# Two expert chunks issued during the attention, a separate region for one of them, and two raw buffers for the last four weight halves

## The chip, the cores and the metric

The kernel runs on one core of one Trainium2 chip. The metric is the device time of one execution in microseconds (us); lower is better. The figures for the kernel before are three runs and one more execution that the hardware profiler recorded.

## The reference, cut to what matters

One transformer layer for 256 tokens of width 1024, all in float32: a gated linear attention and a gating unit side by side, then cross-attention to 256 memory rows, then a mixture of 32 experts.

```
x = x + (gate_a * y_a + gate_b * y_b) @ w_mix_out[l]
mem_n = _rmsnorm(mem, norm_mem_g[l])
x = x + _cross_attn(_rmsnorm(x, norm_x_g[l]), mem_n, w_xq[l], w_xk[l], w_xv[l], w_xo[l])
x = x + _moe(_rmsnorm(x, norm_ffn_g[l]), w_router[l], b_router[l], w_e1[l], b_e1[l], w_e2[l], b_e2[l])
```

`_cross_attn` computes, for four heads of width 256, `softmax(q k^T / 16) v` and multiplies the heads by `w_xo`. `_moe` takes the four best experts of each token; each expert is two matrices, `w_e1[e]` (1024 x 2048) and `w_e2[e]` (1024 x 1024), 12.6 MB together, with a clipped gate between them. All 32 experts are computed, so about 403 MB of expert weights are read in every execution.

## The kernel before, in words

The program has one hand-written instruction list per engine. Semaphores alone order the engines among each other; each engine, and the DMA queue that SP (SyncE) issues, goes through its own list in order.

**The dense part.** The weights of the dense matrices come in 21 pieces (`PIECES`), each of two halves of 1 MB, so 42 halves with numbers n from 0 to 41. Piece `xq1` is halves 36 and 37, `xo0` is 38 and 39, `xo1` is 40 and 41. SP loads half n into one of four raw buffers (`load_half`, profile line L352). ScalarE (ACT) copies it with rounding into a "high" part (`high_part`, L548), GpSimd (POOL) computes the "low" part as the difference (`low_part`, L466) and increments `low_made`, and TensorE (PE) multiplies with both parts (L1224 and L1268). A raw buffer is free again when the low part of the half in it is done, so with `N_RAW_SLOTS` = 4 half n is issued when `low_made` has reached n - 3. The pairs of high and low parts have three buffers of their own, so `high_part(n)` also waits until PE has used half n - 3.

**The attention.** PE computes the scores of heads 0 to 3 (L1413), VectorE (DVE) takes the row maximum (L1018) and scales it with a small operation on `stat` (L1021), ACT takes the exponentials (`soft`, L689), DVE multiplies the probabilities by the reciprocal sums (L1028), PE transposes them (L1202) and multiplies them with the values (`attend`, L1430). In ACT's list the order around the change is: high part 39, two copies, high part 40, `soft(2)`, `soft(3)`. Half 41 has its high part after the four heads. Then PE multiplies by `xo0` and `xo1` (L1224), normalises, computes the router and begins the experts.

**The experts.** An expert is six chunks of 2 MB: c = 0 to 3 of the first matrix (PE at L1551) and 4, 5 of the second (PE at L1584). Eight chunk slots are reused in turn: one is the memory rows' old buffer, one lies in `shared`, two are the four raw buffers taken in twos (`raw_slot(1)` is raw buffers 2 and 3, `raw_slot(0)` is 0 and 1), and four are the old pair buffers and hT. Two more places serve only once, for chunks 3 and 4 of expert 0 (`EXTRA_CHUNKS`). Chunk 3 goes to `from_glu`, the region of `shared` in which the experts' activations will lie. Before, that region overlaps the probabilities of the attention. Chunk 4 goes in two halves to `sgu_vectors` and `side`. SP issues a chunk into a reused slot when PE has used what was in it (`chunk_was_used`); all chunk issues show as L367, chunk 3 as L416.

SP's list before, from half 37 on: halves 38 to 41, each behind its `low_made`; chunk 0 once PE has filled group `vm11`; chunk 1 once `ao3`, the last head, is filled; chunk 3; chunk 2; chunk 5 when all 42 low parts are done; chunks 6 to 9 as the output projection ends; the two halves of chunk 4; then the slots in turn.

Of the kernel before, what the change touches and what calls it, by code (L numbers as in the profile page):

```python
# [44 lines left out]

PIECE_HALF = DC * HALF // 2
N_RAW_SLOTS = 4
N_PAIR_SLOTS = 3
HALF_CHUNK = 2 * D
CHUNK = 2 * HALF_CHUNK  # L50
# [7 lines left out]
EXTRA_CHUNKS = (W1_CHUNKS - 1, W1_CHUNKS)  # L58
# [3 lines left out]
PIECES = ["qk", "v", "r", "sv", "u", "ga0", "ga1", "gb0", "gb1", "pa", "pb", "xk0", "xk1",  # L62
          "mx0", "mx1", "xv0", "xv1", "xq0", "xq1", "xo0", "xo1"]
# [29 lines left out]
def bank_of(group):  # L93
    return INDEX[group] % N_BANKS
# [10 lines left out]
def use_of(group):  # L105

    return INDEX[group] // N_BANKS + 1


def layer_program(nc, a, out):  # L110
    with ExitStack() as ctx:
        def sb(name, shape, dt=F32):
            return ctx.enter_context(nc.sbuf_tensor(name, shape, dt))

        def sem(name):
            return ctx.enter_context(nc.semaphore(name))
# [3 lines left out]

        raw = sb("raw", [P, N_RAW_SLOTS * PIECE_HALF])
        with ExitStack() as early:
            def early_sb(name, shape):
                return early.enter_context(nc.sbuf_tensor(name, shape, F32R))


            pairs = early_sb("pairs", [P, N_PAIR_SLOTS, 2, DC // 2, HALF])
            hT = early_sb("hT", [P, 2, DC, T])
            memT = early_sb("memT", [P, 2, DC, T])

        late = sb("late", [P, 2 * N_PAIR_SLOTS * PIECE_HALF + 4 * DC * T])
        with ExitStack() as early:
# [38 lines left out]
        at = [0]  # L171

        def carve(cols, p=P):
            v = shared[0:p, at[0]:at[0] + cols]
            at[0] += cols
            assert at[0] <= 13 * 1024, at[0]
            return v

        def cut(v, *dims):
            if len(dims) == 2:  # L180
                return v.rearrange("p (a b) -> p a b", a=dims[0])
            return v.rearrange("p (a b c) -> p a b c", a=dims[0], b=dims[1])
# [48 lines left out]
        putT = cut(carve(TT * P), TT, P)  # L231
        gathered = carve(HALF)
        xeT = cut(carve(HALF), 4, P)
        glu_at = at[0]
        glu = carve(HALF)
        lin = carve(HALF)
# [3 lines left out]
        from_glu = shared[:, glu_at:glu_at + CHUNK]  # L240
# [8 lines left out]
        bank_emptied = [sem(f"bank_emptied{b}") for b in range(N_BANKS)]  # L249
        raw_full = [sem(f"raw_full{b}") for b in range(N_RAW_SLOTS)]  # L250
        extra_full = [sem(f"extra_full{b}") for b in range(len(EXTRA_CHUNKS))]
# [12 lines left out]
        s = {n: sem(n) for n in names}  # L264

        block = ctx.enter_context(nc.Block())


        def raw_half(n):
            k = n % N_RAW_SLOTS  # L270
            return raw[:, k * PIECE_HALF:(k + 1) * PIECE_HALF]

        def raw_arrived(eng, n):
            eng.wait_ge(raw_full[n % N_RAW_SLOTS], 16 * (n // N_RAW_SLOTS + 1))

        def pair(m):
            return pairs[:, m % N_PAIR_SLOTS]

        def split_used(eng, m):

            if m % 2 == 0:
                eng.wait_ge(s["first_half_used"], m // 2 + 1)
            else:
                filled(eng, LAST_USE[PIECES[m // 2]])
# [8 lines left out]
        HALVES = 2 * len(PIECES)  # L293
        pair_order = [m % N_PAIR_SLOTS for m in range(HALVES - N_PAIR_SLOTS, HALVES)]
        hT_slot, memT_slot = N_PAIR_SLOTS, N_PAIR_SLOTS + 1

        chunk_slots = ([late_slot(memT_slot), shared[:, 0:CHUNK], raw_slot(1), raw_slot(0)]
                       + [late_slot(q) for q in pair_order] + [late_slot(hT_slot)])
        assert len(chunk_slots) == N_CHUNK_SLOTS and 2 * PIECE_HALF == CHUNK == 2 * DC * T
        assert (HALVES - N_RAW_SLOTS) % N_RAW_SLOTS == 2  # L300

        def turn_of(c):

# [3 lines left out]
        def slot_of(c, step_is_first):  # L307
            return (turn_of(c) if step_is_first else c - len(EXTRA_CHUNKS)) % N_CHUNK_SLOTS
# [15 lines left out]
        def filled(eng, group):  # L324
            eng.wait_ge(bank_filled[bank_of(group)], use_of(group))
# [6 lines left out]
        def piece_source(name):  # L332
            def cols(w, lo):
                return w.rearrange("(c p) n -> p c n", p=P)[:, :, lo:lo + HALF]
            lows = {"qk": 0, "v": OFF_V, "r": OFF_R, "u": OFF_U, "sv": OFF_SV, "ga0": OFF_G,
                    "ga1": OFF_G + HALF, "gb0": OFF_G + D, "gb1": OFF_G + D + HALF}
            if name in lows:
                return cols(w_in[0], lows[name]), DC
            if name in ("pa", "pb"):
                return a["w_proj_a" if name == "pa" else "w_proj_b"][0].rearrange("(c p) n -> p c n", p=P), DC // 2  # L340
            w = {"xk": "w_xk", "xv": "w_xv", "mx": "w_mix_out", "xq": "w_xq", "xo": "w_xo"}[name[:2]]
            return cols(a[w][0], HALF * int(name[2])), DC

        @block.sync
        def _(sp):
            def load_half(n):
                if n >= N_RAW_SLOTS:

                    sp.wait_ge(s["low_made"], n - N_RAW_SLOTS + 1)
                src, c = piece_source(PIECES[n // 2])  # L350
                src = src[:, (n % 2) * (c // 2):(n % 2 + 1) * (c // 2), :]
                sp.dma_start(raw_half(n).rearrange("p (c n) -> p c n", c=c // 2), src).then_inc(  # L352
                    raw_full[n % N_RAW_SLOTS], 16)

            def chunk_source(c, e):

                k = c % CHUNKS
                if k < W1_CHUNKS:
                    rows_ = a["w_e1"][0, e, k * W1_SUB * P:(k + 1) * W1_SUB * P, :]
                    return rows_.rearrange("(p i) n -> p (i n)", i=W1_SUB)  # L360
                k -= W1_CHUNKS
                rows_ = a["w_e2"][0, e, k * W2_SUB * P:(k + 1) * W2_SUB * P, :]
                return rows_.rearrange("(p i) n -> p (i n)", i=W2_SUB)

            def load_chunk(c, e, step_is_first=False):
                slot = slot_of(c, step_is_first)
                sp.dma_start(chunk_slots[slot], chunk_source(c, e)).then_inc(chunk_full[slot], 16)  # L367
# [13 lines left out]
            sp.dma_start(wa2[:], a["gla_w_a2"][0]).then_inc(s["wa2_in"], 16)  # L381
            sp.dma_start(router_bias[:], a["b_router"][0:1, :].to_broadcast([P, N_EXP])).then_inc(s["wr_in"], 16)
            load_half(0)
            load_half(1)
            load_half(2)
# [7 lines left out]
            for n in range(N_RAW_SLOTS, HALVES):  # L393
                load_half(n)
                if n == 2 * PIECES.index("xk0"):

                    filled(sp, "o1")
                    for q in range(4):
                        cols = a["b_e1"][0].rearrange("e (h j n) -> e h j n", h=2, j=2)[:, :, q // 2, :]
                        sp.dma_start(b1_rows[N_EXP * q:N_EXP * (q + 1), :].rearrange("e (h n) -> e h n", h=2),  # L400
                                     cols).then_inc(s["b1_in"], 16)
                if n == 2 * PIECES.index("xv1"):

                    filled(sp, "kT0")
                    sp.wait_ge(s["sv_normed"], 2)
                    sp.dma_start(g_ffn, a["norm_ffn_g"][0:1, :].to_broadcast([P, D])).then_inc(s["gffn_in"], 16)
                    sp.dma_start(g_final, a["norm_final_g"].rearrange("(a d) -> a d", a=1).to_broadcast(
                        [P, D])).then_inc(s["gfin_in"], 16)
                    sp.dma_start(b2, a["b_e2"][0]).then_inc(s["b2_in"], 16)

            filled(sp, "vm11")
            load_chunk(0, 0, True)
            filled(sp, "ao3")
            load_chunk(1, 0, True)
            sp.wait_ge(s["b1_split"], 1)
            sp.dma_start(from_glu, chunk_source(EXTRA_CHUNKS[0], 0)).then_inc(extra_full[0], 16)  # L416
            sp.wait_ge(s["low_made"], HALVES - 2)
            load_chunk(2, 0, True)
            sp.wait_ge(s["low_made"], HALVES)
            load_chunk(5, 0, True)  # L420
            filled(sp, "x210")
# [16 lines left out]
            n = sp.value_load(trips[0:1, 0:1], min_val=GROUPS_OF_EXPERTS, max_val=ROUNDS * GROUPS_OF_EXPERTS)  # L438
# [15 lines left out]
        def _(pool):  # L454
# [7 lines left out]
            def low_part(m):  # L462

                pool.wait_ge(s["high_made"], m + 1)
                high, low = (pair(m)[:, i].rearrange("p c n -> p (c n)") for i in range(2))
                g.tensor_tensor(low, raw_half(m), high, ALU.subtract).then_inc(s["low_made"], 1)  # L466
# [35 lines left out]
        def _(sc):  # L502
# [41 lines left out]
            def high_part(m):  # L544
                if m >= N_PAIR_SLOTS:
                    split_used(sc, m - N_PAIR_SLOTS)
                raw_arrived(sc, m)
                A.activation(pair(m)[:, 0].rearrange("p c n -> p (c n)"), raw_half(m), ACT.Copy).then_inc(  # L548
                    s["high_made"], 1)
# [1065 lines left out]
```

## Time and profile before

| what | value |
|---|---|
| runs | 1243.12, 1241.75, 1241.39 us; median 1241.75 us |
| the profiled execution | 1242.61 us, its span 1240.9 us |
| TensorE busy | 1162.9 us, 94% of the span |
| VectorE, ScalarE, GpSimd busy | 347.0, 279.0, 205.1 us |
| HBM read | 451.79 MB, 365 GB/s over the span |

The span runs from the first to the last instruction of the program; the 1.7 us between it and the time lie around it. The page cuts the span into 40 slices of 31 us. In them the DMA rate is 136 to 313 GB/s up to slice 9, 430 in slice 10, 333, 377 and 413 in the next three, and 427 to 430 from there almost to the end:

```
GB/s 313 170 204 136 178 179 199 192 140 430 333 377 413 430 427 427 429 429 428 428 429 428 427 429 429 429 428 429 428 427 429 428 427 429 430 429 427 429 428 210
```

The dense part ends and the experts begin at about 315 us.

### The profile page before, as it was taken

The numbers are of one execution on the slowest core, as the hardware profiler recorded it, in microseconds if no ns is written. First come the engines' busy times: TensorE is split into PE (matmuls) and PEld (weight loads), VectorE is DVE, ScalarE is ACT, GpSimd is POOL, SyncE is SP. The second block draws the span as 40 slices with busy tenths as digits, with TensorE's granted clock in tenths as the row PEclk, the third lists the DMA queues.
The fourth block names the chain that finished last, engine by engine and source line by source line (L and its number), as shares of the span: only waits on it lengthen the run. The fifth ranks groups of instructions, "written<-read, shape, count | busy, mean of one in ns | idle before, by whom it ended". The sixth has DMA issues, their size and how long they took to land.

```text
span 1240.9 us, 13691 instructions
## 1 busy us (share of the span) xinstructions
PE 1162.9 (94%) x5560; PEld 543.6 (44%) x5560; DVE 347.0 (28%) x672; ACT 279.0 (22%) x392; POOL 205.1 (17%) x66
## 2 busy tenths in 40 slices
PE   6899999998999999999999999999999999999996
PEld 5788898987333333333333333333333333333332
DVE  3843183144222222222222222222222222222222
ACT  5554445533211111111111111111111111111112
POOL 7776777831000000000000000000000000000000
PEclk9999999998999999999999999999999999999999
DMA  8563555539899999999999999999999999999995
GB/s 313 170 204 136 178 179 199 192 140 430 333 377 413 430 427 427 429 429 428 428 429 428 427 429 429 429 428 429 428 427 429 428 427 429 430 429 427 429 428 210
DMA packets 54039, 453.24 MB, mean 365 GB/s; under 512 B 6318, under 2 KB 6876, under 8 KB 29308
## 3 DMA queue, kind: packets, MB, share of 16 engines
q1 hardware_dynamic: 53952, 452.84, 88.7%
q8 instruction: 20, 0.33, 0.1%
q14 instruction: 7, 0.06, 0.0%
q10 hardware_dynamic: 60, 0.02, 0.0%
HBM read 451.79 MB, written 1.05 MB: 365 GB/s over the span
## 4 chain that ended last, share of the span: by engine, by line
PE 71%; DMA 14%; DVE 10%; issue 2%; ACT 2%; POOL 0%; SPq 0%; DVEq 0%; ACTq 0%
PE ps L1551 29%; PE ps L1584 15%; PE ps L1224 11%; DMA raw<-in_w_e 8%; DMA late<-in_w_e 5%; PE ps L1532 4%; PE ps L1268 4%; DVE shared L1174 2%; DVE shared L1171 2%; DVE shared L1168 2%; PE ps L1573 1%; PE ps L1384 1%; PE ps L1541 1%; DVE shared L1169 1%; ACT shared L743 1%
## 5 line engine op out<-in xcount | busy, mean ns | idle before, releaser
L1551 PE MATMUL ps<-late,shared 128*64 128x512 f32 x1248 | 278.6, 596 | 3.4 <-DMA late<-in_w_e 3.4
L466 POOL TENSOR_TENSOR pairs<-raw,pairs 128x2048 fp32r<-128x2048 f32 x42 | 196.0, 4677 | 77.3 <-ACT pairs L548 77.2
L1148 DVE TENSOR_TENSOR rows<-ps,rows 128x512 f32<-128x512 f32 x128 | 79.4, 683 | 414.4 <-PE ps L1532 414.4
L1551 PEld LDWEIGHTS ps<-late,shared 128*64 128x64 f32 x1248 | 85.7, 137 | 180.8 <-issue 171.7
L1584 PE MATMUL ps<-late,shared 128*64 128x512 f32 x640 | 142.6, 596 | 6.5 <-ACT shared L743 6.5
L737 ACT ACTIVATE shared<-shared 128x512 f32<-128x512 f32 x32 | 20.1, 629 | 536.5 <-DVE shared L1168 536.5
L1224 PE MATMUL ps<-pairs,hT 128*128 128x512 f32 x576 | 134.5, 394 | 3.3 <-POOL pairs L466 3.3
L1551 PE MATMUL ps<-raw,shared 128*64 128x512 f32 x528 | 119.0, 596 | 1.9 <-DMA raw<-in_w_e 1.8
L1224 PEld LDWEIGHTS ps<-pairs,hT 128*128 128x128 f32 x576 | 108.8, 190 | 27.0 <-POOL pairs L466 3.7
L1168 DVE TENSOR_SCALAR shared<-ps 128x512 f32<-128x512 f32 x32 | 22.1, 692 | 297.2 <-PE ps L1551 297.2
L548 ACT ACTIVATE pairs<-raw 128x2048 fp32r<-128x2048 f32 x42 | 80.2, 1916 | 68.3 <-PE ps L1224 37.5
L1584 PEld LDWEIGHTS ps<-late,shared 128*64 128x64 f32 x640 | 44.1, 137 | 89.6 <-issue 81.3
L1551 PEld LDWEIGHTS ps<-raw,shared 128*64 128x64 f32 x528 | 36.2, 137 | 78.1 <-issue 72.9
L747 ACT ACTIVATE shared<-ps 128x512 f32<-128x512 f32 x32 | 19.1, 597 | 214.9 <-PE ps L1584 214.9
L1488 PE MATMUL ps<-normed,shared 128*64 128x512 f32 x264 | 65.7, 619 | 1.5 <-DVE shared L1097 1.5
L1532 PE MATMUL ps<-shared 64*128 64x512 f32 x256 | 63.6, 615 | 0.7 <-ACT shared L747 0.7
L1551 PE MATMUL ps<-shared 128*64 128x512 f32 x272 | 61.8, 596 | 1.8 <-DMA shared<-in_w_e 1.8
L1584 PE MATMUL ps<-raw,shared 128*64 128x512 f32 x240 | 53.2, 595 | 1.8 <-ACT shared L743 1.8
L1573 PE MATMUL ps<-ident,shared 128*128 128x128 f32 x128 | 21.0, 287 | 31.1 <-DVE shared L1174 31.1
L721 ACT ACTIVATE shared<-ps 128x512 f32<-128x512 f32 x33 | 35.7, 1083 | 24.5 <-PE ps L1488 24.5
L1532 PEld LDWEIGHTS ps<-shared 64*128 64x128 f32 x256 | 22.0, 186 | 41.6 <-issue 40.1
L1573 PEld LDWEIGHTS ps<-ident,shared 128*128 128x128 f32 x128 | 13.4, 140 | 59.3 <-DVE shared L1174 59.3
(203 smaller groups left out, 898.1 us busy)
## 6 DMA issues: line engine op xcount, KB each, us to landing
late<-in_w_e SPq DMA_DIRECT2D x118, 2048.0 KB, 24.4
raw<-in_w_e SPq DMA_DIRECT2D x48, 2048.0 KB, 24.0
shared<-in_w_e SPq DMA_DIRECT2D x25, 2048.0 KB, 23.6
raw<-in_w_in SPq DMA_DIRECT2D x18, 1024.0 KB, 5.1
raw<-in_w_xk SPq DMA_DIRECT2D x4, 1024.0 KB, 5.5
raw<-in_w_mix_out SPq DMA_DIRECT2D x4, 1024.0 KB, 5.0
raw<-in_w_xv SPq DMA_DIRECT2D x4, 1024.0 KB, 5.6
raw<-in_w_xq SPq DMA_DIRECT2D x4, 1024.0 KB, 5.0
```

Of the source, the lines that this page charges most:

```text
L466: g.tensor_tensor(low, raw_half(m), high, ALU.subtract).then_inc(s["low_made"], 1)
L548: A.activation(pair(m)[:, 0].rearrange("p c n -> p (c n)"), raw_half(m), ACT.Copy).then_inc(s["high_made"], 1)
L721: A.activation(by_part, in_rows, ACT.Copy).then_inc(s["gather_copied"], 1)
L1148: V.tensor_tensor(rows[:, t, c], ps[:, SCATTER_BANKS[k], :], rows[:, t, c], ALU.add).then_inc(s[f"y_added{k}"], 1)
L1168: V.tensor_scalar(glu, ps[:, HIDDEN_BANKS[0], :], LIMIT, None, ALU.min).then_inc(s["glu_made"], 1)
L1224: last = M.matmul(bank(group), lhs[:, a, half * (DC // 2) + c, t * P:(t + 1) * P], w[:, b, c, :], start=first, stop=final, skip_group_chec ...
L1268: last = M.matmul(bank(group)[:, i * T:(i + 1) * T], w[:, b, c, f * P:(f + 1) * P], rhs[:, a, half * (DC // 2) + c, :], start=first, stop= ...
L1488: last = M.matmul(ps[64 * j:64 * j + 64, GATHER_BANK, :], take[:, t, :], normed[:, t, j * HALF:(j + 1) * HALF], start=t == 0, stop=t == 1, ...
L1532: M.matmul(ps[:, SCATTER_BANKS[k], :], putT[q, t, :], y_rows[q, :], start=k not in with_bias, stop=True, skip_group_check=True).then_inc(s ...
L1551: last = M.matmul(ps[64 * j:64 * j + 64, HIDDEN_BANKS[h], :], xeT[:, c % 2 * W1_SUB + part, j0:j0 + SLOTS], w[:, h * D + j * HALF:h * D + ...
L1573: last = M.transpose(ps[:, PUT_BANK, q * P:(q + 1) * P], act[:, q * P:(q + 1) * P], ident[:])
L1584: last = M.matmul(ps[64 * j:64 * j + 64, Y_BANK, :], actT[:, part, c * SLOTS:(c + 1) * SLOTS], w[:, j * HALF:(j + 1) * HALF], start=c + pa ...
```

## The change

It has three parts. First, halves 38 to 41 go through two raw buffers instead of four: 38 and 40 into buffer 0, 39 and 41 into buffer 1. Each of them waits for the low part of the half that was last in its buffer, so 38 waits until `low_made` is 37 (it was 35), 39 until 38 (36), 40 until 39 (37), 41 until 40 (38). Raw buffers 2 and 3 are free after half 35. Second, the activations of the experts (`glu`, `lin`, `sig`, `act` and what follows) move up in `shared` so that `from_glu` begins at column 7 * 1024, behind the probabilities. Third, SP issues chunk 3 right behind half 37 (once the biases' `b1_split` is done), and chunk 0 and chunk 2 right behind half 39, ahead of halves 40 and 41. Chunk 0 was issued behind half 41 before; chunks 3 and 2 behind chunk 1.

```
+LAST_HALVES = 4
...
         xeT = cut(carve(HALF), 4, P)
+        at[0] = 7 * 1024
         glu_at = at[0]
...
+        def raw_slot_of(n):
+            return n % 2 if n >= 2 * len(PIECES) - LAST_HALVES else n % N_RAW_SLOTS
+
+        def earlier_in_slot(n):
+            return [m for m in range(n) if raw_slot_of(m) == raw_slot_of(n)]
+
         def raw_half(n):
-            k = n % N_RAW_SLOTS
+            k = raw_slot_of(n)
             return raw[:, k * PIECE_HALF:(k + 1) * PIECE_HALF]
 
         def raw_arrived(eng, n):
-            eng.wait_ge(raw_full[n % N_RAW_SLOTS], 16 * (n // N_RAW_SLOTS + 1))
+            eng.wait_ge(raw_full[raw_slot_of(n)], 16 * (len(earlier_in_slot(n)) + 1))
...
+        raw1_left = max(n for n in range(HALVES) if raw_slot_of(n) >= 2) + 1
...
             def load_half(n):
                 if n >= N_RAW_SLOTS:
-                    sp.wait_ge(s["low_made"], n - N_RAW_SLOTS + 1)
+                    sp.wait_ge(s["low_made"], earlier_in_slot(n)[-1] + 1)
...
+                if n == 2 * PIECES.index("xo0") - 1:
+
+                    sp.wait_ge(s["b1_split"], 1)
+                    sp.dma_start(from_glu, chunk_source(EXTRA_CHUNKS[0], 0)).then_inc(extra_full[0], 16)
+                if n == 2 * PIECES.index("xo0") + 1:
+
+                    filled(sp, "vm11")
+                    load_chunk(0, 0, True)
+                    sp.wait_ge(s["low_made"], raw1_left)
+                    load_chunk(2, 0, True)
...
-            filled(sp, "vm11")
-            load_chunk(0, 0, True)
             filled(sp, "ao3")
             load_chunk(1, 0, True)
-            sp.wait_ge(s["b1_split"], 1)
-            sp.dma_start(from_glu, chunk_source(EXTRA_CHUNKS[0], 0)).then_inc(extra_full[0], 16)
-            sp.wait_ge(s["low_made"], HALVES - 2)
-            load_chunk(2, 0, True)
             sp.wait_ge(s["low_made"], HALVES)
             load_chunk(5, 0, True)
```

## Rows read from the trace of the kernel before

**Rows 1.** The chain of waits that ended last: start us, us, what.

```profile
69.92 10.93 PE ps L1224 x48
333.46 7.09 PE ps L1584 x32
948.18 31.59 DMA raw<-in_w_e
```

**Rows 2.** The waits of PE from 315 to 940 us: total, times, longest.

```profile
PE ps L1573 <- DVE shared L1174: 21.4, 22, 1.0
PE ps L1584 <- ACT shared L743: 5.9, 22, 0.3
```

**Rows 3.** One window: busy time by engine, then TensorE's granted clock, DMA share, GB/s.

```profile
335.00:340.00 5.00, 5.00 (x26) 1.58 (x22) 0.00 (x0) 0.00 (x0) 0.00 (x0) 1.00 0.05 20
```

**Rows 4.** SP's issues in time: start us, us, engine line, what.

```profile
240.07 0.37 SPq L352 DMA_DIRECT2D raw<-in_w_xo  x1
...
245.76 0.50 SPq L367 DMA_DIRECT2D late<-in_w_e  x1
...
274.73 11.56 SPq L367 DMA_DIRECT2D raw<-in_w_e  x2
...
340.59 0.33 SPq L367 DMA_DIRECT2D raw<-in_w_e  x1
```

**Rows 5.** DMA view of 240 to 241 us: the issue, KB, us to landing.

```profile
raw<-in_w_xo SPq DMA_DIRECT2D x1, 1024.0 KB, 4.9
```

**Rows 6.** DMA view of 245 to 246.5 us: half 41 and chunk 0.

```profile
late<-in_w_e SPq DMA_DIRECT2D x1, 2048.0 KB, 9.6
raw<-in_w_xo SPq DMA_DIRECT2D x1, 1024.0 KB, 5.2
```

**Rows 7.** DMA view of 340 to 341 us: the chunk issued at 340.59.

```profile
raw<-in_w_e SPq DMA_DIRECT2D x1, 2048.0 KB, 7.7
```

**Rows 8.** DMA views at 3.6 and 5.5 us: halves 0 and 3.

```profile
raw<-in_w_in SPq DMA_DIRECT2D x1, 1024.0 KB, 8.4
...
raw<-in_w_in SPq DMA_DIRECT2D x1, 1024.0 KB, 14.6
```

**Rows 9.** ACT in time; the value in brackets is idle time before it.

```profile
244.95 1.90 ACT L548 ACTIVATE pairs<-raw 128x2048 fp32r<-128x2048 f32 x1
...
259.92 1.90 ACT L548 ACTIVATE pairs<-raw 128x2048 fp32r<-128x2048 f32 x1
...
266.61 0.47 ACT L689 ACTIVATE shared<-ps,stat 128x256 f32<-128x256 f32 x1 [4.79 <-DVE stat L1021]
```

**Rows 10.** POOL in time: low parts 38, then 39 and 40.

```profile
246.93 4.58 POOL L466 TENSOR_TENSOR pairs<-raw,pairs 128x2048 fp32r<-128x2048 f32 x1 [1.61 <-ACT pairs L548]
257.50 9.05 POOL L466 TENSOR_TENSOR pairs<-raw,pairs 128x2048 fp32r<-128x2048 f32 x2 [5.99 <-ACT pairs L548]
```

**Rows 11.** DVE in time, in the attention.

```profile
262.75 3.82 DVE L1021 TENSOR_SCALAR stat<-stat 128x2 f32<-128x2 f32 x1
...
267.86 0.69 DVE L1028 TENSOR_TENSOR shared<-shared,stat 128x512 f32<-128x512 f32 x1
```

**Rows 12.** PE in time, in the attention.

```profile
260.10 3.62 PE L1413 MATMUL ps<-shared,side 128*128 128x256 f32 x16
...
268.61 0.66 PE L1202 MATMUL ps<-ident,shared 128*128 128x128 f32 x4 [1.44 <-DVE shared L1028]
...
273.49 1.72 PE L1224 MATMUL ps<-pairs,hT 128*128 128x512 f32 x6
```

**Rows 13.** POOL near 55 us.

```profile
52.11 9.60 POOL L466 TENSOR_TENSOR pairs<-raw,pairs 128x2048 fp32r<-128x2048 f32 x2 [6.41 <-ACT pairs L548]
```

**Rows 14.** DVE near 57 us.

```profile
57.90 4.37 DVE L883 TENSOR_TENSOR shared<-shared 128x512 f32<-128x512 f32 x1
```

**Rows 15.** PE near 57 us, and the window 58 to 60 us.

```profile
56.70 12.78 PE L1224 MATMUL ps<-pairs,hT 128*128 128x512 f32 x48 [3.27 <-POOL pairs L466]
...
58.00:60.00 2.00, 2.00 (x6) 1.52 (x6) 2.00 (x1) 0.03 (x1) 2.00 (x1) 0.50 0.87 291
```

More of the change, by code:

```diff
@@ L299, in layer_program @@
         assert len(chunk_slots) == N_CHUNK_SLOTS and 2 * PIECE_HALF == CHUNK == 2 * DC * T
-        assert (HALVES - N_RAW_SLOTS) % N_RAW_SLOTS == 2
+        raw1_left = max(n for n in range(HALVES) if raw_slot_of(n) >= 2) + 1
         def turn_of(c):
@@ L352, in load_half @@
                 sp.dma_start(raw_half(n).rearrange("p (c n) -> p c n", c=c // 2), src).then_inc(
-                    raw_full[n % N_RAW_SLOTS], 16)
+                    raw_full[raw_slot_of(n)], 16)
             def chunk_source(c, e):
```

## The prediction

> **What bounds the kernel now.** I read the time by slices first, then the chain of waits, then PE's waits in the expert part, then SP's issues with their landings. The slices show the DMA at 427 to 430 GB/s from about 400 us on. The chain agrees for the end: at 948.18 it goes over to a wait of 31.6 us on an expert chunk, and such waits return to the end [rows 1]. So the end is the last chunk's landing plus a fixed tail, and that landing is the last moment at which the DMA stream was held up, plus the bytes left over its rate.
>
> Where was it last held up? Not in the attention. From 335 to 340 us the DMA moves 20 GB/s, a share of 0.05, while PE is busy for all 5.00 us [rows 3]: the queue is empty, since all slots are full and PE has not freed one. The next issue is at 340.59 [rows 4], when the second matrix of expert 0 has been used (333.46 + 7.09 = 340.55 [rows 1]); it lands 7.7 us later [rows 7], at 348.3. A stream short of bandwidth would have had no such hole. From there on PE waits for nothing but DVE and ACT, and for no DMA, until 940 [rows 2]. So in this stretch PE sets when slots come free, and the stream starts from PE's clock, not from the loads before it. Two consequences. Loads that are done earlier than PE needs them bring nothing. And what delays or advances PE before 340 moves the end by the same amount. The question for this change is thus only what it does to PE between 225 and 315 us.
>
> **The chunks moved forward: 0.** Chunks 3, 0 and 2 are 2 MB each. At the stream's rate one takes 2.1 MB / 428 GB/s = 4.9 us. All three are in place before PE wants them: before, as PE waits for no DMA from 315 on [rows 2], and after, as they come earlier. The slots they occupy are the same, and the first reuse waits for PE as before. What would be late next is nothing: the stream still stops at the full slots before 340. The move of the activations to column 7 * 1024 adds no instruction; it only removes the overlap with the probabilities. Cost 0.
>
> **The waits added on SP.** Chunk 3 goes out behind half 37; its wait on `b1_split` concerns DVE work done long before, in the dense part. It takes 4.9 us of an idle queue around 230 us and is gone before half 38 is issued. Chunk 0's wait was already over at 245.76, where it was issued straight behind half 41 [rows 4], and chunk 2's (`low_made` 36) is weaker than half 38's own (37). Behind these on SP's list stand halves 40 and 41, and on them hang ACT, POOL and PE.
>
> **Halves 38 and 39: about 0.1, hidden.** Half 38 now waits for 37 low parts, which is what half 40 waited for before. Half 40 was issued at 240.07 [rows 4], so half 38 goes there and lands 4.9 us later [rows 5], at 245.0. Its high part began at 244.95 [rows 9], so it moves by 0.1 to 0.3 us. Low part 38 ended at 246.93 + 4.58 = 251.5 and POOL then stood idle for 5.99 us [rows 10], which hides that. Half 39 takes the place of half 41, in the queue just ahead of 245.76, and lands near 250.5, some 5 us before its high part is due (POOL takes it at 257.50 [rows 10]). Cost 0; it would be 0.3 if that cover were gone.
>
> **Half 40: late.** It waits for low part 38 and is issued at about 251.7. By then chunks 0 and 2 are in the queue. Chunk 0 lands at 245.76 + 9.6 = 255.4 [rows 4, 6], chunk 2 4.9 later at 260.3, and half 40 behind it. A half in a full queue takes 2.7 us: halves 0 and 3, issued at 3.6 and 5.5, land at 12.0 and 20.1, so 8.1 for three [rows 8]. That gives 263.0. Its high part began at 259.92 [rows 9]; it now begins at 263.05 and ends at 264.95. This alone costs nothing on ACT: `soft(2)`, next on its list, began at 266.61 [rows 9].
>
> But low part 40 on POOL moves too. It takes 4.6 us; it ran from about 262.0 to 257.50 + 9.05 = 266.55 [rows 10]. Now it runs from 265.0 to 269.6. What it does to DVE can be read in two places. The 128x2 operation L1021 at 262.75 took 3.82 us and ended at 266.57, with POOL's end at 266.55 [rows 10, 11]. And L883, a product of two 128x512 operands in `shared`, began at 57.90 and took 4.37 us instead of the 0.69 of the same shape at L1028 [rows 11, 14]; it ended at 62.27, 0.56 us after POOL's low part (52.11 + 9.60 = 61.71 [rows 13]). So a DVE operation of these kinds, issued while a low part runs, ends about when the low part does, or 0.56 later for 128x512.
>
> Before, the stall fell on L1021 of head 2. After, POOL is idle at 262.75: L1021 of head 2 takes its short time, and ACT begins `soft(2)` at 264.95 instead of 266.61. It gains 1.7 us there, and loses more one step later: L1028 of head 2, of the stalled kind, cannot start before two exponentials of 0.47, so about 266.0, when low part 40 already runs. It ends at 269.6 + 0.56 = 270.15 instead of 267.86 + 0.69 = 268.55 [rows 11]. That is **+1.6 us**. PE waits for exactly this operation: its transposes began at 268.61 after 1.44 us of idleness [rows 12]. Everything behind goes with it: the heads, `xo0` at 273.49 [rows 12] becomes 275.1, the router, the experts' start, the issue at 340.59.
>
> A second small stall is possible: L1021 of head 3. PE's scores end at 260.10 + 3.62 = 263.7 [rows 12]; the row maximum takes 0.7, so L1021 runs at 264.5, 0.5 us before low part 40. If half 40 lands half a microsecond earlier, this one is caught, `soft(3)` waits until 269.3, and the gain on L1028 of head 2 is spent on head 3; the sum stays within 0.3 us.
>
> The Trainium skill has a rule on the order assumed here: "DMA: Bandwidth & Descriptors", section "Two DMAs through the same engine are not ordered", says that descriptors of one queue start in order but may complete otherwise, and that nothing orders the 16 engines. If that let half 40 overtake chunk 2, the shift would be gone; it is the third case below.
>
> **Half 41** needs low part 39 (262.0 [rows 10], unmoved), is issued at 262.1 and lands behind half 40, at about 267. Its high part waits for PE's use of half 38, after 275. Cost 0. PE wants half 40 only in `xo1`, 10.9 us [rows 1] after 275.1, against 269.6: 16 us in hand.
>
> **Sum.** Against the profiled execution: span 1240.9 + 1.6 = 1242.5, with the 1.7 around it 1244.2. That execution took 1242.61, 0.86 more than the median of the runs; on the median it is 1241.75 + 1.6 = **1243.4 us**. The bounds: at least 0 (no stall, PE unmoved); at most 1.6 plus 0.3 (head 3) plus about 0.9 for a landing of half 40 that is a little later, as each microsecond there is one at the end.
>
> **The rivals.** *The lengthened pause costs PE's clock (slower).* PE's pause before the transposes of heads 2 and 3 grows from 1.44 to 3.0 us, near the 3.27 us before 56.70, behind which the clock stood at 0.50, the 1.2 GHz level, in the window 58 to 60 [rows 15]; the 48 matmuls there took 12.78 us against 10.93 at full clock [rows 1, 15]. The same here would add 1.85: 1241.75 + 1.6 + 1.85 = 1245.2. For it: the two pauses are nearly as long. Against: it is 0.3 us shorter, PE was fully busy on both sides, and short transposes follow at once. It decides from the point where the pause reaches that of 56.70. The Trainium skill's "TensorE: Matmul & The Clock Gate", section "Why this matters for your kernels", has the rule to leave no long idle gaps between bursts, as the clock falls back to half; the rows at 57 us agree.
>
> *No shift.* Half 40 lands by 261 (it overtakes, or chunk 2 goes faster), so low part 40 ends by 267.3 and costs no more than before. Then PE is unmoved: 1241.8. For it: a 1 MB transfer alone takes 4.9 us [rows 5], so half 40 by itself would land at 256.6. Against: chunk 0, issued 0.4 us behind half 41, landed 4.8 us after it (255.4 against 245.4 + 5.2) [rows 6], in order and at the full rate.
>
> *The stream is the bound from the attention on (faster).* If the end hung on bytes and not on slots, two chunks fewer behind 274 us would be 2 x 4.9 = 9.8 us, less the hole that opens: chunk 1 alone, issued near 275.5, lands at 283.2, and chunk 5 is issued at 274.73 + 11.56 + 1.6 = 287.9 [rows 4], 7.7 us on the way where the stream would have gone through; chunks 3 and 2 filled just this. The balance is 9.8 - 7.1 = 2.7: 1239.1. For it: the rate of 430 in slice 10. Against: the empty queue at 335 to 340 [rows 3], which wipes out whatever came before.
>
> **How the numbers follow.** Chances: the forecast 0.50, the clock 0.22, no shift 0.18, the stream 0.07, 0.03 for costs not seen. A measurement can tell about 0.2%, 2.5 us, from no change. The forecast at +1.6 lies within it; I give a fifth of its chance, 0.10, to a landing late enough to pass 2.5. So slower 0.22 + 0.10 + part of the rest = 0.33; faster 0.07 and the noise, 0.08; same 0.59. The forecast's own range is 1242.6 to 1244.5. The whole range takes in no shift, with the 0.9 us by which the runs differ, and the clock case: 1241.0 to 1245.8.
>
> **What would show it.** Right: half 40 landing at about 263; POOL's low part 40 from 265 to 269.6; L1021 of head 2 at about 0.17 us, L1028 of head 2 at about 4 us; PE's pause before L1202 at 3 us; the first L1551 1.6 us later; SP's issue at 340.59 now at 342.2; the end as much later. Wrong: a busy DMA at 337 to 342, a wait of PE on DMA before 900, or expert chunks whose issue times do not follow PE.

## The result and the profile after

| kernel | runs | median us | ratio to before | 95% interval |
|---|---|---|---|---|
| before | 6 | 1241.94 | 1 | |
| changed | 6 | 1246.12 | 1.0033 | 1.0021 to 1.0045 |
| changed, again on another occasion | 12 | 1246.39 | 1.0034 | 1.0022 to 1.0046 |

The changed kernel is slower by 4.2 us. 1243.4 with no measurable change was forecast, so the direction was missed and the time lies above the range by 0.3 us.

Two executions of the changed kernel were recorded. The first took 1244.14 us (span 1242.4), but its start was luckier: PE reached the scores of heads 2 and 3 at 256.63, 3.5 us before the kernel before (260.10, [rows 12]); the difference was there when the 48 matmuls of [rows 15] ended, at 66.05 us instead of 69.48, because they began 1.9 us earlier and the clock did not fall behind the pause ahead of them, which was 2.65 us here. Within 0.02 us of the kernel before at the scores is the second one, span 1244.5, time 1246.26. The rows of after below are of that one where nothing else is said. Lines are shifted: 12 behind the dense part (L1028 is now L1040, L1202 is L1214, L1224 is L1236), 8 in SP's list.

The chain of waits through the attention (start us, us, what) answers to [rows 1, 12]:

```profile
251.63 12.59 DMA raw<-in_w_xo
...
264.30 1.91 ACT pairs L560
266.21 0.92 ACT shared L701 x4
...
267.35 4.00 DVE shared L1040
271.35 0.04 issue
271.39 1.92 PE ps L1214 x8
273.31 4.49 PE ps L1442 x16
277.80 21.81 PE ps L1236 x96
```

Half 40 is issued at 251.63 and takes 12.59 us to land, its high part follows, then the exponentials, then L1040 of head 2 with 4.00 us, then PE. No DMA stood between PE and its work here before. The engines in time, as in [rows 10 to 12]:

```profile
266.29 4.50 POOL L478 TENSOR_TENSOR pairs<-raw,pairs 128x2048 fp32r<-128x2048 f32 x1 [4.24 <-ACT pairs L560]
...
262.74 0.17 DVE L1033 TENSOR_SCALAR stat<-stat 128x2 f32<-128x2 f32 x1
...
267.35 3.99 DVE L1040 TENSOR_TENSOR shared<-shared,stat 128x512 f32<-128x512 f32 x1
271.26 0.15 DVE L1038 RECIPROCAL stat<-stat 128x2 f32<-128x2 f32 x1
271.45 0.69 DVE L1040 TENSOR_TENSOR shared<-shared,stat 128x512 f32<-128x512 f32 x1
...
271.39 1.92 PE L1214 MATMUL ps<-ident,shared 128*128 128x128 f32 x8 [4.24 <-DVE shared L1040]
```

Low part 40 ends at 266.29 + 4.50 = 270.79 and L1040 of head 2 at 267.35 + 3.99 = 271.34, 0.55 later. The stall of [rows 11] has moved from the scaling of the maximum (L1033, now 0.17 us) to the product. PE pauses 4.24 us where it paused 1.44. Behind the pause its clock falls; a window of the changed kernel (columns as in [rows 3]) and the same of before:

```profile
270.00:276.00 6.00, 4.61 (x17) 3.62 (x18) 4.68 (x7) 0.00 (x0) 0.79 (x1) 0.72 0.00 0
```

```profile
270.00:276.00 6.00, 6.00 (x29) 5.06 (x28) 3.33 (x6) 1.20 (x2) 0.00 (x0) 1.00 0.23 49
```

The mean of 0.72 is a piece at the 1.2 GHz level (0.50 in 272 to 274) between pieces at 2.4. In the first recorded execution, too, the clock was 0.50 from 270 to 272 behind a pause of 4.30 us:

```profile
268.01 1.67 PE L1214 MATMUL ps<-ident,shared 128*128 128x128 f32 x8 [4.30 <-DVE shared L1040]
...
270.00:272.00 2.00, 2.00 (x6) 1.54 (x6) 1.67 (x3) 0.00 (x0) 0.00 (x0) 0.50 0.00 0
```

So in the second execution `xo0` begins at 277.45 instead of 273.49, 3.96 us later: 2.78 us of wait and 1.2 of clock. The stream stands still as before, only later ([rows 3, 4]):

```profile
339.00:343.00 4.00, 4.00 (x22) 1.41 (x20) 0.00 (x0) 0.00 (x0) 0.00 (x0) 1.00 0.06 20
```

```profile
343.91 0.33 SPq L375 DMA_DIRECT2D raw<-in_w_e  x1
```

Here the issue that stood at 340.59 is 3.3 us later, and the last wait on a chunk ends at 1218.3 instead of 1214.7, 3.6 later, as much as the span has grown.

Neither is the full 3.96. What goes with the difference is a second stretch at half clock that every recorded execution has, between `xo0` and the experts' start. In the kernel before it lasts 13.7 us, from about 299 to 313; one window of it (columns as above):

```profile
300.00:305.00 5.00, 4.91 (x24) 4.54 (x23) 2.31 (x10) 2.27 (x4) 0.00 (x0) 0.50 1.01 429
```

Its length differs from one execution to the next, and with it the time from the first product of `xo0` to the end of the last wait on a chunk: 942.2 to 942.6 us in the three executions with 17.1 us at half clock, 941.2 and 941.9 with 13.7, 940.9 to 941.0 in the four with 10.2, and 939.1 and 939.0 with 6.8 and 3.4. The second execution of the changed kernel has 10.2 us, the kernel before 13.7. So two executions can differ by up to 3.6 us behind the place of the change. No run here shows what sets this length.

### The profile page after: what moved, and what is told of

It is laid out like the page before. It is cut to its first block, busy times and chain, and to the rows that moved or that the text cites. A ratio compares the mean times of both kernels' runs of the same rounds, so it can differ in the third digit from the quotient of the medians.

```text
span 1242.4 us, 13691 instructions
## 1 busy us (share of the span) xinstructions
PE 1164.2 (94%) x5560; PEld 544.4 (44%) x5560; DVE 346.0 (28%) x672; ACT 279.1 (22%) x392; POOL 205.7 (17%) x66
## 4 chain that ended last, share of the span: by engine, by line
PE 70%; DMA 15%; DVE 10%; ACT 2%; issue 2%; POOL 1%; DVEq 0%; SPq 0%; ACTq 0%
PE ps L1563 29%; PE ps L1596 15%; PE ps L1236 11%; DMA raw<-in_w_e 8%; DMA late<-in_w_e 5%; PE ps L1544 4%; PE ps L1280 3%; DVE shared L1186 2%; DVE shared L1183 2%; DVE shared L1180 2%; PE ps L1585 1%; PE ps L1396 1%; PE ps L1553 1%; DVE shared L1181 1%; ACT shared L755 1%
## 5 line engine op out<-in xcount | busy, mean ns | idle before, releaser
L1236 PE MATMUL ps<-pairs,hT 128*128 128x512 f32 x576 | 133.0, 391 | 2.6 <-POOL pairs L478 2.6
L1236 PEld LDWEIGHTS ps<-pairs,hT 128*128 128x128 f32 x576 | 107.6, 188 | 25.9 <-POOL pairs L478 3.1
```

The lines of the kernel that those rows point to most:

```text
L1236: last = M.matmul(bank(group), lhs[:, a, half * (DC // 2) + c, t * P:(t + 1) * P], w[:, b, c, :], start=first, stop=final, skip_group_chec ...
```

## The experiments

The stretch from the start of the scores of heads 2 and 3 to the first product of `xo0`, read from PE's timeline, is 13.39 to 13.41 us in the four executions with a pause of about 1.44, and 11.73 in both that have the late high part; it stands beside each median. The changed kernel's is 17.37 us in its second execution, which the table shows, and 17.72 in its first. The kernels ran on three occasions, and each ratio is against runs of the kernel before made beside them. The runs also list their mean granted clock. A straight line through the 74 runs of the kernel before, made beside all these kernels, gives 0.87 us for each 0.001 of clock. The last column is a kernel's mean distance from that line, so its cost at equal clock, with its standard error. It takes out all that the clock costs, wherever in the execution, so also the 1.2 us of the changed kernel's own pause.

| kernel | median us | ratio (95% interval) | stretch us | at equal clock us |
|---|---|---|---|---|
| before | 1241.9 to 1242.1 | 1 | 13.39 | 0 |
| changed (again) | 1246.39 | 1.0034 (1.0022 to 1.0046) | 17.37 | +3.0 (0.2) |
| chunks 0, 2 behind half 41 | 1241.58 | 0.9991 (0.9982 to 1.0001) | 13.39 | -0.3 (0.3) |
| chunk 0 ahead of half 40 only | 1242.35 | 0.9995 (0.9984 to 1.0006) | 13.41 | -0.3 (0.2) |
| chunk 3 early only | 1240.52 | 0.9991 (0.9981 to 1.0002) | 13.41 | 0.0 (0.3) |
| changed, high 40 late | 1239.06 | 0.9972 (0.9961 to 0.9984) | 11.73 | -1.2 (0.2) |
| before, high 40 late | 1239.08 | 0.9972 (0.9961 to 0.9983) | 11.73 | -1.0 (0.2) |
| low 40 in quarters | 1241.52 | 0.9992 (0.9980 to 1.0005) | 13.77 | +0.8 (0.2) |
| pause filled, 14 | 1244.70 | 1.0027 (1.0015 to 1.0039) | 17.78 | +4.4 (0.2) |
| pause filled, 9 | 1243.58 (before 1240.27 beside it) | 1.0027 (1.0015 to 1.0039) | 16.38 | +3.3 (0.2) |

### Chunks 0 and 2 behind half 41

```
-                if n == 2 * PIECES.index("xo0") + 1:
+                if n == 2 * PIECES.index("xo1") + 1:
```

> The changed kernel with chunks 0 and 2 issued behind half 41 instead of ahead of half 40; chunk 3 early and the two raw buffers stay. Theory (half 40 queues behind two chunks, so low part 40 on GpSimd holds up the product L1028 of head 2): half 40 lands about 5 us after its issue, its high part runs straight after the copies as in the kernel before, and the whole loss of 4.2 us is gone: ratio to before 0.999 to 1.001. Rival (the two raw buffers or the early chunk 3 cost it): the loss stays, ratio near 1.003.

The loss is gone, with two raw buffers and the early chunk 3 in place. Half 40 lands 5.0 us after its issue at 249.95, so at 254.9. PE in time:

```profile
266.81 0.66 PE L1214 MATMUL ps<-ident,shared 128*128 128x128 f32 x4 [1.44 <-DVE shared L1040]
```

The pause is back at 1.44. So the loss sits in the two DMAs ahead of half 40, not in the other parts.

### Chunk 0 ahead of half 40, chunk 2 behind half 41

```
                     load_chunk(0, 0, True)
+                if n == 2 * PIECES.index("xo1") + 1:
+
                     sp.wait_ge(s["low_made"], raw1_left)
                     load_chunk(2, 0, True)
```

> The changed kernel with chunk 0 ahead of half 40, but chunk 2 behind half 41. Theory: half 40 lands 4.9 us earlier than in the changed kernel, before ACT is ready for it, so nothing is lost: ratio 0.999 to 1.001, PE's pause before the transposes of heads 2 and 3 back at 1.4 us. Rival (each chunk ahead of it costs its share): half of the loss, ratio 1.0015.

Half 40 takes 6.5 us, from 249.81 to 256.3, and ACT wants it at 258.02 here, so nothing is lost:

```profile
266.73 0.65 PE L1216 MATMUL ps<-ident,shared 128*128 128x128 f32 x4 [1.45 <-DVE shared L1042]
```

The cost is not proportional to what stands ahead. It needs a landing behind ACT's turn (259.92 in [rows 9]), and chunk 2 is what takes it past; at which landing between these two kernels the cost begins, no run shows.

### High part 40 behind the exponentials, in both kernels

```
             high_parts("xo0", 1)
...
-            high_parts("xo1", 0)
             soft(2)
             soft(3)
+            high_parts("xo1", 0)
```

> The changed kernel with ACT's high part 40 moved behind soft(2) and soft(3), so that low part 40 runs after the two DVE products of heads 2 and 3. Loads and waits of SP as in the changed kernel. Theory (the loss comes only through GpSimd's low part against DVE, and through PE's clock after the pause): PE's pause falls below 0.5 us, no clock drop behind it, and the time is 1 to 3 us below the kernel before: ratio 0.9975 to 0.9995. Rival (the late halves or the busier queue cost by themselves): ratio 1.001 or more.

> The kernel before with the same reordering on ACT alone. Theory: it also removes the 3.8 us stall of L1021 in the kernel before, and as early chunks bring nothing, it comes out the same as the changed kernel with the reordering, within 0.1%: 1 to 3 us below before. Rival (the early chunks bring a gain once the stall is gone): the changed kernel with the reordering is at least 2 us faster than this one.

Both come out at 1239.1 us, 2.9 below the kernel before and some 7 below the changed one. Only 1.7 of the 2.9 lie in the stretch (11.73 against 13.39). The rest goes with the clock: these runs have a mean of 0.993 and 0.994, those of the kernel before beside them 0.991, and in the two recorded executions the half clock ahead of the experts lasted 10.2 and 3.4 us instead of 13.7. Whether the new order brings that or chance does, no run here shows. SP's list is untouched in each. In the changed kernel with this order half 40 still lands 12.4 us after its issue. PE and DVE of it:

```profile
265.36 1.04 PE L1214 MATMUL ps<-ident,shared 128*128 128x128 f32 x8
266.81 3.72 PE L1442 MATMUL ps<-shared 128*128 128x256 f32 x16 [0.41 <-DVE shared L809]
```

```profile
261.11 0.17 DVE L1033 TENSOR_SCALAR stat<-stat 128x2 f32<-128x2 f32 x1
262.83 0.17 DVE L1033 TENSOR_SCALAR stat<-stat 128x2 f32<-128x2 f32 x1
263.10 0.69 DVE L1040 TENSOR_TENSOR shared<-shared,stat 128x512 f32<-128x512 f32 x1
264.29 0.69 DVE L1040 TENSOR_TENSOR shared<-shared,stat 128x512 f32<-128x512 f32 x1
...
265.94 4.53 POOL L478 TENSOR_TENSOR pairs<-raw,pairs 128x2048 fp32r<-128x2048 f32 x1 [5.52 <-ACT pairs L560]
```

Low part 40 starts behind both products; neither is stalled, and PE's only wait is 0.41 us. This settles two things. The late half costs nothing when its low part does not meet DVE's operations. And once that is mended, the three early chunks bring nothing that can be seen: 1239.06 against 1239.08, equal stretches, and at equal clock -1.2 (0.2) against -1.0 (0.2), which leaves room for less than 1 us, and not for the 2 of the rival in the expectation.

### Low part 40 in quarters

```
-                g.tensor_tensor(low, raw_half(m), high, ALU.subtract).then_inc(s["low_made"], 1)
+                parts = 4 if m == 2 * PIECES.index("xo1") else 1
+                n = PIECE_HALF // parts
+                for i in range(parts):
+                    c = slice(i * n, (i + 1) * n)
+                    last = g.tensor_tensor(low[:, c], raw_half(m)[:, c], high[:, c], ALU.subtract)
+                last.then_inc(s["low_made"], 1)
```

> The changed kernel with low part 40 as four GpSimd instructions of 128x512 instead of one of 128x2048. Theory (a GpSimd instruction holds DVE's operation off until that instruction ends, not until the tensor is done): L1028 of head 2 waits for the running quarter only and ends about 2 us earlier than in the changed kernel, PE's pause falls from 4.3 to about 2 us, total 1.5 to 3 us below the changed kernel, ratio to before 0.9995 to 1.002. Rival (DVE waits for low_made or for ACT, not for the instruction): L1028 ends where it did, ratio 1.003.

```profile
267.18 0.75 DVE L1045 TENSOR_TENSOR shared<-shared,stat 128x512 f32<-128x512 f32 x1
...
268.09 1.52 DVE L1045 TENSOR_TENSOR shared<-shared,stat 128x512 f32<-128x512 f32 x1
...
266.12 5.84 POOL L482 TENSOR_TENSOR pairs<-raw,pairs 128x512 fp32r<-128x512 f32 x4 [4.29 <-ACT pairs L565]
```

The product runs amid the low part: 0.75 us for head 2, during which the first quarter gives way to the second, and 1.52 for head 3, which began inside the second quarter and ended at 269.61, 0.5 us behind it. `low_made` comes only with the fourth quarter, at 271.96, so DVE waited for the single instruction and not for the tensor. GpSimd pays in turn: 5.84 us for four instead of 4.50 for one. The median is 4.9 us below the changed kernel, more than the 1.5 to 3 expected, of which 3.6 lie in the stretch. The pause falls into two, and the clock is 1.00 behind them:

```profile
267.98 0.66 PE L1219 MATMUL ps<-ident,shared 128*128 128x128 f32 x4 [1.05 <-DVE shared L1045]
269.66 0.66 PE L1219 MATMUL ps<-ident,shared 128*128 128x128 f32 x4 [1.02 <-DVE shared L1045]
...
270.00:276.00 6.00, 6.00 (x29) 5.00 (x28) 3.47 (x6) 1.20 (x2) 1.96 (x2) 1.00 0.22 44
```

### PE's pause filled with matmuls

```
             attend(1)
+            start_group("pT2")
+            for n in range(14):
+                M.matmul(bank("pT2")[:, 0:T], side_T[:, 0, 0:P], kT[:, 0, :], start=True, stop=True)
             probs_T(2)
```

> The changed kernel with 14 matmuls of 128x256 on PE (0.23 us each, 3.2 us) that write into the bank of head 2's transposes ahead of them and are overwritten: PE works through most of its 4.3 us pause and waits as long as before for the product L1028. Theory (of the 4.2 us loss about 2.8 is the longer wait and 1.4 the half clock behind it): the clock stays at 1.00 behind the pause, the attention behind it takes 4.9 us instead of 6.3, and the total is 1.2 to 1.7 us below the changed kernel, ratio to before 1.0015 to 1.0025. Rival (the whole loss is the wait): no difference to the changed kernel, ratio 1.003.

Mis-sized: the 14 show as 28 rows and took 6.21 us, not 3.2, and PE came to the transposes 1.8 us after they could start. So the stretch is 17.78 us, longer than the changed kernel's, and yet the median is 1.7 us lower: that difference lies outside the stretch and says nothing of the pause. The same with `range(9)`:

> As the kernel with the filled pause, but 9 matmuls instead of 14. The 14 took 6.2 us (0.44 each, not 0.23) and ran 1.8 us over the pause; 9 take 4.0 us and fit in the 4.2 us. Theory (2.8 us of the loss is the wait, 1.2 to 1.5 the half clock behind it): clock 1.00 behind the pause, PE's first matmul of xo0 about 3 us after that of the kernel before instead of 4.0, total 1.2 to 1.5 us below the changed kernel: ratio to before 1.0015 to 1.0028. Rival (the loss is the wait alone): as the changed kernel, 1.0034.

```profile
265.59 4.05 PE L1460 MATMUL ps<-shared,side 128*128 128x256 f32 x18
270.18 1.46 PE L1214 MATMUL ps<-ident,shared 128*128 128x128 f32 x8 [0.54 <-DVE shared L1040]
271.69 3.72 PE L1442 MATMUL ps<-shared 128*128 128x256 f32 x16
...
270.00:276.00 6.00, 5.63 (x28) 4.60 (x29) 4.16 (x8) 1.15 (x2) 0.00 (x0) 1.00 0.00 0
```

L1040 of head 2 takes as long as before the filling (4.00 us), the clock stays at 1.00 in the window 270 to 276, and the heads take 3.72 us instead of 4.70. The stretch is 16.38, so 1.0 us of the 4.0 was clock and 3.0 wait. The stretch of the recorded executions carries this; the medians do not, as 1.0027 and 1.0034 have overlapping intervals. Nor does the mean clock by itself: it is 0.993 over the runs of either filled kernel against 0.990 for the changed one, but 0.991 and 0.993 for the kernel before beside them, which has no fall of the clock in this place.

### Chunk 3 alone

```
-LAST_HALVES = 4
+LAST_HALVES = 0
```

Chunks 0 and 2 also went back to their places of before.

> Only the first part of the change: the region behind the probabilities and chunk 3 issued behind half 37; chunks 0 and 2 and the four raw buffers as in the kernel before. Theory (a chunk loaded earlier brings nothing, since the stream stops at full slots near 337 us, and nothing stands behind it): same as before, ratio 0.999 to 1.001. Rival (each chunk taken out of the busy stretch behind 274 us saves up to 4.9 us): ratio 0.998 or less.

Same as before within the interval; the stretch is 13.41 and the cost at equal clock 0.0 (0.3). A gain of 2.5 us or more is excluded, one of 0.5 is not.

The repeat of the changed kernel had this expectation:

> The changed kernel again, on the same chip as the three experiments beside it, to compare with them: 3.5 to 4.5 us above before, ratio 1.003.

## Why the prediction was wrong, step by step

**The bound: right.** The end hangs on when PE gets through the stretch between 225 and 345 us and not on the bytes loaded before. The empty stretch of [rows 3] moved with PE, and the two reordered kernels, one with the three chunks early and one without, have the same time. The rival in which the stream is the bound is refuted by that pair. (Its 7.1 us for the hole is not worked out; its own times give 283.2 to 287.9 and 2.8 more to land, 7.5, so a gain of 2.3 and not 2.7. Nothing hangs on it.) What the forecast left out of this stretch is the half clock ahead of the experts, 13.7 us long before and 10.2 in the execution of after: of the 3.96 us at `xo0`, 3.3 were left at the issue and 3.6 at the end.

**Region, chunk 3, halves 38 and 39, half 41: right, 0.** The first experiment has all of these and measures 0.9991.

**The lock: right in place and price.** Low part 40 holds L1040 of head 2 up to 0.55 us behind its own end (0.56 was taken from [rows 13, 14]). The quarters show that DVE waits for the single GpSimd instruction and not for the tensor. The Trainium skill has it in "SBUF — State Buffer", section "SBUF: two separate sides": GpSimd and VectorE share a pair of ports as an exclusive lock, held for a whole instruction, against VectorE operations in a two-port mode, or with two SBUF inputs where the GpSimd operation reads SBUF. The two stalled kinds agree with it, and the price here is 3.3 us on an operation of 0.69. Not every VectorE operation pays: the reciprocal L1038 at 267.15, inside low part 40, took 0.17 us.

**Half 40's landing: mis-sized by 1.2 us.** This is the first step that failed. The term "chunk 2 4.9 later at 260.3, half 40 at 263.0" was 261.8 and 264.2: chunk 2 landed 6.5 us behind chunk 0 and not 4.9, and half 40 2.4 behind that and not 2.7. Between 6.2 and 6.6 us stood in all six recorded executions with chunk 2 in this place, and 4.9 in the two in which it was issued behind half 41. The DMA view of 257 to 261 us shows what else was in the engines then:

```profile
q1 hardware_dynamic: 358, 1.53, 94.4%
q8 instruction: 1, 0.02, 1.7%
q14 instruction: 1, 0.01, 0.5%
```

Two packets of instructions, one of 16 KB that takes about 1.1 us of one of the 16 engines (1.7% of 16 engines for 4 us). If a chunk counts as landed only when the slowest of them is done, which no view here shows, one busy engine delays it whole. The larger packet comes between 254 and 260 us in all eleven recorded executions. In the kernel before it came at 256 us, when the expert chunk ahead of it was already in place (chunk 0 landed at 255.4). That fits in time and size; no kernel here moved a fetch, so the cause is argued and not shown. As the forecast said, each microsecond there is one at the end: the wait grew by 2.8 and not 1.6.

**The clock: judged too unlikely.** This is the second step that failed, and it hangs on the first. The rival "the lengthened pause costs PE's clock" had 0.22 and 1.85 us. It came true in both recorded executions, for 1.0 to 1.5 us. The argument against it was that the pause, at 3.0 us, would be 0.3 shorter than that of 56.70. With the landing 1.2 us later the pause was 4.2, and the argument fell with the first error. The two terms were not independent, and the chances treated them so.

**The sum.** 2.8 of wait and 1.2 of clock are 4.0, beside the 4.2 measured. That they meet so closely is in part luck, as the half clock ahead of the experts alone moves single executions by up to 3.6 us. The wait by itself would just have passed the 2.5 us that a measurement can tell, at 1244.6; the clock took it to 1245.8, the top of the range, and the measured median is 0.3 above.

## What to carry to other kernels

Before a bulk load is put ahead of a small one, ask which instruction waits for the small one and what that instruction collides with when it comes late: here 2 MB too many cost 4 us through a GpSimd operation that meets a VectorE product, while the loads gained nothing because full slots stopped the stream later anyway. When a wait is priced, price the engine that it leaves idle as well: pauses of 4.2 and 4.3 us had half the clock behind them here, two of about 1 us had not, so both terms rise together. And look for the stall that is already there: moving one ACT instruction behind two heads' exponentials freed VectorE from the same lock and made the kernel before 2.9 us faster (ratio 0.9972, 0.9961 to 0.9983), 1.7 of it in the attention. Last, compare a small change in the stretch that it touches, too: of the 2.9 us here, and of the 4.9 that the quarters took off, over 1 us lay elsewhere.

## What the runs showed of the hardware that was not expected

- A 2 MB chunk landed 6.2 to 6.6 us behind its predecessor in a full queue, instead of 4.9, where an instruction fetch lay in the same stretch. That the fetch is the cause is not shown.
- Runs of one kernel differ by their mean granted clock: over 74 runs of the kernel before it went from 0.989 to 0.997 and the time from 1244.9 to 1237.4, 0.87 us for each 0.001. What remains around the line is 0.7 us.
- PE worked at half clock ahead of the experts in all eleven recorded executions, for 3.4 to 17.1 us, and the time from `xo0` to the last wait on a chunk went from 939.0 to 942.6 with it.
- One float32 matmul of 128x256 from `side` and `kT` took 0.44 us of PE and stands as two rows.
